# A narrower second top-16 search, ranks turned into key numbers by one operation per rank, and ScalarE's gelu moved one tile later

## The reference

```python
s1 = q[:, :, 0] @ sub_keys1.T        # 256 tokens, 8 heads, 128 keys
s2 = q[:, :, 1] @ sub_keys2.T
v1, i1 = lax.top_k(s1, 16)
v2, i2 = lax.top_k(s2, 16)
cand = v1[..., :, None] + v2[..., None, :]            # 16 x 16 sums per head
top, ci = lax.top_k(cand.reshape(..., 256), 16)
idx = i1[ci // 16] * 128 + i2[ci % 16]                # one of 16384 experts
gate = softmax(top)
act = gelu(x . expert_u[idx])
out = sum(gate * act * expert_v[idx])
```

## Time and profile before

| | us |
|---|---|
| median of 3 runs | 2029.18 |
| the profiled execution | 2028.88 |
| its span, first to last instruction | 2027.0 |
| TensorE (PE) busy | 2004.3 |
| VectorE (DVE) busy | 1488.2 |
| ScalarE (ACT) busy | 1061.8 |
| GpSimd (POOL) busy | 1029.8 |

### The profile page before, as it was taken

How to read it: one execution, slowest core, us unless ns; L and a number is a source line. 1 busy time by engine, 2 the same in 40 slices (tenths; PEclk the granted TensorE clock), 3 DMA queues, 4 the chain that set the end, 5 groups by cost and what they waited for, 6 DMA issues and landing times.

```text
span 2027.0 us, 39960 instructions
## 1 busy us (share of the span) xinstructions
PE 2004.3 (99%) x12788; PEld 1819.2 (90%) x12788; DVE 1488.2 (73%) x3096; ACT 1061.8 (52%) x1746; POOL 1029.8 (51%) x425
## 2 busy tenths in 40 slices
PE   9999999999999999999999999999999999999998
PEld 7999998899999888888889999888999998888887
DVE  2855169988887888888639450799888878888886
ACT  5644555567776333333466444555677753333333
POOL 6898779787775000000278988798777740000001
PEclk8999999999999999999999999999999999999999
DMA  8355557675666787878774556676666567787775
GB/s 256 129 194 188 183 186 235 212 226 198 197 195 195 244 239 242 242 240 242 240 208 143 192 174 199 194 235 215 213 197 199 197 203 243 240 241 241 241 242 175
DMA packets 172128, 429.62 MB, mean 212 GB/s; under 512 B 19156, under 2 KB 83957, under 8 KB 171510
## 3 DMA queue, kind: packets, MB, share of 16 engines
q1 hardware_dynamic: 171588, 425.56, 66.5%
q10 hardware_dynamic: 434, 2.63, 0.3%
HBM read 392.79 MB, written 35.32 MB: 211 GB/s over the span
## 4 chain that ended last, share of the span: by engine, by line
PE 93%; DVE 3%; issue 1%; POOL 1%; ACT 1%; DMA 1%; DVEq 0%; POOLq 0%; ACTq 0%; SPq 0%
PE bank L1300 40%; PE bank L1563 33%; PE bank L1549 9%; PE bank L1551 5%; PE bank L1614 3%; POOL halves L545 1%; PE bank L1529 1%; DVE area L1155 0%; DVE area L1159 0%; DVE area L1162 0%; PE bank L1439 0%; DMA ring<-in_stream 0%; PE bank L1395 0%; DVE act L1235 0%; DMA x<-in_x 0%
## 5 line engine op out<-in xcount | busy, mean ns | idle before, releaser
L545 POOL TENSOR_TENSOR halves<-ring,halves 128x1024 fp32r<-128x1024 f32 x412 | 1024.2, 2498 | 975.7 <-DVE coef L1243 683.0
L626 ACT ACTIVATE halves<-ring 128x1024 fp32r<-128x1024 f32 x668 | 705.2, 1057 | 684.7 <-PE bank L1563 414.1
L1300 PE MATMUL bank<-hT,halves 128*128 128x256 f32 x6048 | 751.8, 283 | 1.9 <-DVE hT L921 1.7
L1300 PEld LDWEIGHTS bank<-hT,halves 128*128 128x128 f32 x6048 | 737.2, 192 | 4.4 <-DVE hT L921 2.1
L1563 PE MATMUL bank<-halves,coef 128*128 128x512 f32 x3000 | 681.5, 389 | 0.0
L1563 PEld LDWEIGHTS bank<-halves,coef 128*128 128x128 f32 x3000 | 562.7, 188 | 117.4 <-issue 0.5
L1223 DVE TENSOR_TENSOR halves<-ring,halves 128x1024 fp32r<-128x1024 f32 x256 | 315.5, 1233 | 12.7 <-ACT halves L626 10.2
L1549 PE MATMUL bank<-hT,halves 128*128 128x512 f32 x896 | 312.2, 395 | 3.0 <-POOL halves L545 3.0
L1551 PE MATMUL bank<-hT,halves 128*128 128x256 f32 x896 | 248.6, 277 | 0.0
L1549 PEld LDWEIGHTS bank<-hT,halves 128*128 128x128 f32 x896 | 168.1, 188 | 42.7 <-issue 3.6
L1551 PEld LDWEIGHTS bank<-hT,halves 128*128 128x128 f32 x896 | 168.3, 188 | 0.0
(11 more groups left out here) (168 smaller groups left out, 1375.0 us busy)
## 6 DMA issues: line engine op xcount, KB each, us to landing
ring<-in_stream SPq DMA_DIRECT2D x668, 512.0 KB, 4.0
held_blocks<-act SPq DMA_DIRECT2D x244, 128.0 KB, 1.8
act<-held_blocks SPq DMA_DIRECT2D x244, 128.0 KB, 3.0
area<-rel_scratch SPq DMA_DIRECT2D x16, 128.0 KB, 5.4
area<-in_gains SPq DMA_DIRECT2D x4, 512.0 KB, 4.1
x_home<-x ACTq DMA_DIRECT2D x2, 1024.0 KB, 4.2
x<-x_home SPq DMA_DIRECT2D x2, 1024.0 KB, 8.0
area<-in_params SPq DMA_DIRECT2D x2, 640.0 KB, 7.6
```

Source lines behind the costliest of these rows:

```text
L545: pool.tensor_tensor(halves[:, s, 1, :], ring[:, s, :], halves[:, s, 0, :].bitcast(F32), ALU.subtract)\
L626: a.activation(halves[:, s, 0, :], ring[:, s, :], ACT.Copy).then_inc(hi_done, 1)
L1300: i = pe.matmul(o, stationary[a], moving[b], start=begin and n == 0, stop=end and n == len(TERMS) - 1)
```

## The change

The first of the two layers and the second are changed alike.

- **Sums.** Of the 16 x 16 sums of a head, 112 are formed: the first 4 ranks of the first list with all 16 of the second, and the other 12 with the first 4 (a sum at ranks a and b, counted from 1, has at least a x b - 1 sums not below it). Four additions take the place of two. The second search runs over 112 columns in place of 256.
- **Ranks.** With two kinds of rows the split of the index takes two shifts, three copies to float (in SBUF; the two of before went to PSUM) and four fused operations. A rank then becomes a number by 16 fused operations per list, each `(rank == r) * number r` on 256 elements for both token tiles, and two sums of 16 terms per list. 7 folds stand in this part where 12 stood.
- **ScalarE.** For tile n it makes the high side of tile n + 4 and then takes the gelu of tile n - 1. The exponential moves from ahead of the high side of tile 48 to behind that of tile 44 and the gelu of tile 39. The rounds behind it are written out where a loop was.

SP, GpSimd and TensorE have the code of before.

```diff
--- before.py
+++ after.py
@@ -78,7 +78,11 @@
 assert T_PU % RING == 0 and PARKED % RING == 0 and HELD % RING == 0 and NK % RING == 0 and TAIL == RING == 4
 MAIN = NK - EARLY
 GAIN_AT = 12
-EXP_AT = 11
+EXP_AT = 10
+WIDE = 4
+NARROW = 4
+CAND = WIDE * TOPK + (TOPK - WIDE) * NARROW
+assert (WIDE + 1) * (NARROW + 1) > TOPK and WIDE * TOPK == 64
 SEL_AT = 2
 assert SETS == HELD
 HIS = NT - 2
@@ -122,7 +126,7 @@
 NBANK = 8
 NGV = sum(who == "V" for _, who in PLAN)
 NGA = NG - NGV
-NCHAIN = 59
+NCHAIN = 54
 NROOT = 5
 
 
@@ -270,12 +274,13 @@
         row = part(TT, PH, 2, NK)
         val = part(TT, PH, 2, TOPK)
         idx = part(TT, PH, 2, TOPK, dt=U32)
-        cand = part(TT, PH, TOPK, TOPK)
+        cand = part(TT, PH, CAND)
         top = part(TT, PH, TOPK)
         ci = part(TT, PH, TOPK, dt=U32)
         ca = part(TT, PH, TOPK, dt=U32)
         cb = part(TT, PH, TOPK, dt=U32)
-        eq = part(PH, TOPK, TOPK)
+        eq = part(TOPK, S)
+        caf, cbf = part(S), part(S)
         sel = part(3, TT, P)
         summed = part(2, S)
         used[0] = max(used[0], used_mix)
@@ -294,7 +299,7 @@
         key1T, key2T = (bank[0][:, c * S:(c + 1) * S] for c in range(2))
         weightT, weight_low = (bank[1][:, c * S:(c + 1) * S] for c in range(2))
         idf = bank[6][:, :].rearrange("p (t h c r) -> p t h c r", t=TT, h=PH, c=2)
-        caf, cbf = (bank[7][:, c * S:(c + 1) * S].rearrange("p (t h r) -> p t h r", t=TT, h=PH) for c in range(2))
+        c0, c4, c2 = (eq[:, n, :] for n in range(3))
 
         act_row = act[:, :, :].rearrange("p s t -> p (s t)")
         relv = act_row[0:HEADS, 0:NDIST]
@@ -777,19 +782,39 @@
                 high_up_to(T_PU + RING - 1)
 
                 a.activation(stat[:, 13:14], one, ACT.Gelu_apprx_tanh)
-                def turn(r, s):
+                def next_high(r, s):
 
                     a.wait_ge(tiles_used, l * NT + r * RING + (T_PU + s + 1))
                     high(r * RING + (T_PU + RING + s), s)
-                    park(r, s)
-
-                with a.Fori(0, EXP_AT) as r:
+
+                def turn(r, s):
+
+                    next_high(r, s)
+                    if s > 0:
+                        park(r, s - 1)
+                    else:
+                        park_last(r)
+
+                def park_last(r):
+
+                    a.wait_ge(sides_added, l * PARKED + r * RING)
+                    a.wait_ge(held_stored[1], l * (8 * (EARLY - 2)) + r * (8 * RING))
+                    a.activation(act[:, 1, :], summed[:, 1, :], ACT.Gelu_apprx_tanh).then_inc(act_done, 1)
+
+                next_high(0, 0)
+                for s in range(1, RING):
+                    turn(0, s)
+                with a.Fori(1, EXP_AT) as r:
                     for s in range(RING):
                         turn(r, s)
+                next_high(EXP_AT, 0)
+                park_last(EXP_AT)
                 a.wait_ge(shifted_ready, l + 1)
                 a.activation(sel[:, 2], sel[:, 2], ACT.Exp).then_inc(gexp_ready, 1)
                 a.activation(stat[:, 13:14], one, ACT.Gelu_apprx_tanh)
-                with a.Fori(EXP_AT, PARKED // RING - 1) as r:
+                for s in range(1, RING):
+                    turn(EXP_AT, s)
+                for r in range(EXP_AT + 1, PARKED // RING - 1):
                     for s in range(RING):
                         turn(r, s)
                 for s in range(RING):
@@ -801,6 +826,7 @@
                         a.activation(weight[:, :, :], weight_hi.bitcast(F32).rearrange("p (n u) -> p n u", u=FOUR)[:, :, 2:],
                                      ACT.Copy).then_inc(weights_hi, 1)
                     turn(PARKED // RING - 1, s)
+                park_last(PARKED // RING)
 
                 def hold(i):
 
@@ -1112,14 +1138,16 @@
 
                 for t in range(TT):
                     fold()
-                    i = v.tensor_tensor(cand[:, t], val[:, t, :, 0, :].unsqueeze(3).to_broadcast([P, PH, TOPK, TOPK]),
-                                        val[:, t, :, 1, :].unsqueeze(2).to_broadcast([P, PH, TOPK, TOPK]), ALU.add)
+                    for a0, many, width, at in ((0, WIDE, TOPK, 0), (WIDE, TOPK - WIDE, NARROW, WIDE * TOPK)):
+                        sums = cand[:, t, :, at:at + many * width].rearrange("p h (a b) -> p h a b", a=many)
+                        i = v.tensor_tensor(sums, val[:, t, :, 0, a0:a0 + many].unsqueeze(3).to_broadcast([P, PH, many, width]),
+                                            val[:, t, :, 1, 0:width].unsqueeze(2).to_broadcast([P, PH, many, width]), ALU.add)
                 then_search(i)
                 fold()
                 pairs = [(t, h) for t in range(TT) for h in range(PH)]
                 for k in range(2):
                     ks = slice(8 * k, 8 * k + 8)
-                    flat = [cand[:, t, h].rearrange("p a b -> p (a b)") for t, h in pairs]
+                    flat = [cand[:, t, h, :] for t, h in pairs]
                     for n, ((t, h), f) in enumerate(zip(pairs, flat)):
                         i = v.max(top[:, t, h, ks], f)
                         if n < len(pairs) - 1:
@@ -1144,23 +1172,31 @@
                     i = v.tensor_tensor(gate[:, t], top[:, t], top[:, t, :, 0:1].to_broadcast([P, PH, TOPK]), ALU.subtract)
                 i.then_inc(shifted_ready, 1)
 
-                v.tensor_scalar(ca.rearrange("p t h j -> p (t h j)"), ci.rearrange("p t h j -> p (t h j)"), 4, None,
-                                ALU.logical_shift_right)
-                link(v.tensor_scalar(cb.rearrange("p t h j -> p (t h j)"), ci.rearrange("p t h j -> p (t h j)"), 15, None,
-                                     ALU.bitwise_and))
-                v.tensor_copy(caf.rearrange("p t h r -> p (t h r)"), ca.rearrange("p t h r -> p (t h r)"))
-                link(v.tensor_copy(cbf.rearrange("p t h r -> p (t h r)"), cb.rearrange("p t h r -> p (t h r)")))
+                flat = [z.rearrange("p t h j -> p (t h j)") for z in (ci, ca, cb)]
+                v.tensor_scalar(flat[1], flat[0], 4, None, ALU.logical_shift_right)
+                link(v.tensor_scalar(flat[2], flat[0], 2, None, ALU.logical_shift_right))
+                for o, z in zip((c0, c4, c2), flat):
+                    i = v.tensor_copy(o, z)
+                link(i)
+                fold()
+                link(v.scalar_tensor_tensor(caf, c2, float(WIDE - WIDE * TOPK // NARROW), c4, ALU.add, ALU.max))
+                v.scalar_tensor_tensor(c4, caf, -float(TOPK), c0, ALU.mult, ALU.add)
+                link(v.scalar_tensor_tensor(c2, caf, -float(NARROW), c0, ALU.mult, ALU.add))
+                link(v.scalar_tensor_tensor(cbf, c2, float(WIDE * NARROW - WIDE * TOPK), c4, ALU.add, ALU.max))
                 for c, rank in ((0, caf), (1, cbf)):
+                    for r in range(TOPK):
+                        numbers = idf[:, :, :, c, r].rearrange("p t h -> p (t h)").unsqueeze(2).to_broadcast([P, TT * PH, TOPK])
+                        i = v.scalar_tensor_tensor(eq[:, r, :].rearrange("p (h j) -> p h j", j=TOPK), rank.rearrange("p (h j) -> p h j", j=TOPK),
+                                                   float(r), numbers, ALU.is_equal, ALU.mult)
+                        if r % 6 == 5:
+                            fold()
+                    link(i)
                     for t in range(TT):
-                        link(v.tensor_tensor(eq, rank[:, t].unsqueeze(3).to_broadcast([P, PH, TOPK, TOPK]),
-                                             iota[:, 0:TOPK].unsqueeze(1).unsqueeze(1).to_broadcast([P, PH, TOPK, TOPK]),
-                                             ALU.is_equal))
-                        fold()
-                        link(v.tensor_tensor(eq, eq, idf[:, t, :, c, :].unsqueeze(2).to_broadcast([P, PH, TOPK, TOPK]),
-                                             ALU.mult))
-                        fold()
-                        link(v.tensor_reduce(sel[:, c, t].rearrange("p (h j) -> p h j", h=PH), eq, AX.X, ALU.add))
-                        fold()
+                        i = v.tensor_reduce(sel[:, c, t], eq[:, :, t * P:(t + 1) * P].rearrange("p r j -> p j r"), AX.X, ALU.add)
+                        if t == 0:
+                            fold()
+                    link(i)
+                assert EXP_AT * RING <= folds[0] <= PARKED - 2, folds[0]
                 v.wait_ge(gexp_ready, l + 1)
                 gs = small[:, 0:16].rearrange("p (t h) -> p t h", t=TT)
                 link(v.tensor_reduce(gs, gate, AX.X, ALU.add))
```

## The result

The kernel after takes a median of **2057.79 us** (2056.1 to 2059.16, 4 runs) beside 2029.64 us (2028.71 to 2030.52, 4 runs) for the kernel before: a ratio of 1.0138, 95% interval 1.0121 to 1.0156. That is 28 us slower, where the forecast said 12; the time lies 0.8 us above the end of the range. The profiled execution took 2059.16 us, its span is 2057.3, 30.3 above the span of before.

The account below looks back on a forecast made before the run. TensorE, busy 99% of the span, was taken as the bound. Loop, exponential, one-hots and part 2 gave 9.5 us a layer against 2.7, +6.8, taken as 5.9: +11.8 in two layers, 2041.0 us, range 2026 to 2057.

Parts of the forecast that it names:

- The bound: TensorE's gaps in the parked tiles, 2.7 us a layer and 5.4 in all, are the most the change can gain.
- Part 1: Search over 112 sums on VectorE: saves 16 us of VectorE a layer, worth nothing on TensorE.
- rival D: Search of 112 columns costs as one of 256: 12 us of VectorE stay, time as forecast; no chance of its own.
- Part 2: Ranks to numbers on VectorE: 7 folds for 12 and operations behind GpSimd make TensorE wait 1.5 us a layer.
- Part 3: Gelu one tile later on ScalarE delays SP's stores and the loads behind them; expected to decide the time.
- the loop: High side, gelu, store, load, high side two tiles on: 5.83 us against TensorE's 5.56, losing 0.27 per pair.
- The steps from tile 35: Sign in the parked tiles: TensorE waits for GpSimd's low sides in steps from about tile 35, above all behind the exponential.
- The exponential: Moved to tile 44 on ScalarE: finds its input ready, costs 3.4 us less 1.5 of slack, so 2.0 a layer.
- C: Rival, much slower: VectorE's operations behind GpSimd lose 8 us more, or layer 1 keeps 4.2 us landings; 2053 us, chance 0.21.
- B: Rival, no change: loads land about 3.4 us after issue, lateness stays inside the lead; 2029 to 2030 us, chance 0.17.
- A: Rival, faster: loads land within 3.3 us, late starts never add up; 2024.8 us, chance 0.12.

Follow-up runs that it names:

- the best version: Kernel before with 112 sums, 15 folds for 19 ahead of the shifted gates, 15 for 12 behind, exponential ahead of tile 40's high side: 2024.81 us, ratio 0.9977.

## Why the prediction was right or wrong

**The bound: nearly right.** The gaps were 2.7 us a layer, and the best version took 2.5 to 2.6 out of each parked stretch. But that is 1.84 of gaps and 0.7 of busy time behind them, which the bound left out; the 0.9 at the one-hots stayed.

**Part 1: right in its worth, wrong in its size.** Index, maximum and replacement fell from 419 to 269, 413 to 259 and about 410 to 258 ns: 12 us, as worked out, and rival D is refuted. But the four sums took 7.5 us (estimated 2.0), three of the four behind low sides of GpSimd. It did not matter: the folds are pinned in the program, and VectorE's spare time became waiting. Ahead of its folds it stood idle for 30.7 us, where the earlier trace rows have 11.8:

```profile
L1101 DVE TENSOR_REDUCE area<-bank 128x256 f32<-128x512 f32 x56 | 38.4, 688 | 30.7 <-ACT act L780 17.5 <-PE bank L1587 6.8 <-ACT act L802 5.6
```

**Part 2: the step that failed.** The sum's term for part 2 was 1.5 us a layer; VectorE's part alone cost 9 (18.4 in all). The forecast had the right wait, 7 folds in a section too long for four banks, but made the section 32.5 us from the shift on, where 38.1 were measured, and charged too little for its length. Three errors lie on top of each other, beside the count of folds itself (below).

- The four sums over ranks were taken at the 2.28 us of another layout of the terms. They measured 3.8: 6.1 us a layer that no row of before could show, but for which a bound ("another distance between terms") should have stood.
- The 3 us for operations behind GpSimd measured 3.3 (copies 1.8 over their estimate, first fused 1.5), and the subtraction ahead of them another 1.3. Their size was nearly right, but they were priced at 0.5 us. The banks' cover was already used up, so by the forecast's own rule 3 us of VectorE cost 3 us of TensorE. That was an error of arithmetic.
- The sum had each gap at its length, while behind some of them the clock fell to half for a few us. For VectorE's part alone that is 2.8 us of the 9 in each parked stretch.

The rule of part 2 ranks the kernels with 7 folds against the rest, and no more. Written for a section that is measured from the subtraction on, TensorE waits for its length + 1.5 - 0.9 - 2.78 for each fold and one more - 7.3 of cover. The gaps measured stand in two columns, since a second wait shows beside the one for folds:

| kernel | section, us | folds | by the rule | gaps ahead of the transposes | at the transposes |
|---|---|---|---|---|---|
| before | 40.6 | 12 | below 0 | 1.5 (exponential) | 0.3 |
| after | 39.9 | 7 | 11.0 | 9.7 / 7.8 | 0 |
| after, later store | 41.3 | 7 | 12.4 | 8.1 / 7.9 | 0 |
| VectorE's part alone | 39.4 | 7 | 10.5 | 8.2 / 7.9 | 0 |
| before with 7 folds | 37.3 | 7 | 8.4 | 6.6 / 6.5 | 0 |
| VectorE's part, 11 folds | 41.7 | 11 | 1.7 | 0.4 / 0.5 | 2.5 / 2.4 |
| 112 sums, new split | 44.9 | 13 | below 0 | 3.0 | 1.7 |
| the same, exponential earlier | 44.2 | 13 | below 0 | 0 | 5.9 |
| before, exponential earlier | 40.5 | 12 | below 0 | 0 | 2.4 |
| shift behind fold 36 | 47.4 | 15 | below 0 | 0 | 0 |

For the kernels with 7 folds the rule is 1 to 4.5 us too high. With the forecast's own 29.5 + 3 us, and 0.6 for the subtraction, it gives 4.2, not 1.5.

Where the folds are close enough, the section's end decides: the transposes ahead of tile 54 need it. The shift starts 111.8 us behind the first parked matmul, and 54 tiles at 2.775 us end at 149.9. So a section behind fold 40 may last about 38 us. The two kernels that have an earlier exponential and no other gap fit that: 44.2 and 40.5 us would make 6.2 and 2.5 of waiting, and 5.9 and 2.4 were measured. With the shift behind fold 36, 100.7 us in, a section of 47.4 is over in time.

**The missing folds, not the slow sums, are the root.** The kernel before, with none of the new operations, lost 15 us by 7 folds for 12; the change's own operations lost 5.7 with 11. Five folds are 13.9 us of TensorE's pace. Most of what is left there are the 2.5 / 2.4 us at the transposes, the section's length.

**Part 3: mechanism right, place wrong, the size in part luck.** Two of the signs named came: waits for `ring<-in_stream` in dozens of places (46 in a layer) and 4.2 / 2.7 us at the one-hots for the 3.9 foretold. One sign was badly put: the load comes 2.1 us, not 6, behind the high side that sets it off; it is the whole loop that takes 5.8.

What the forecast gave the loop, the exponential and the one-hots together was 8.0 against 2.7, +5.3 a layer; on top of VectorE's part the late gelu cost 9.9 us in both layers, 5.0 each. That the two agree is luck: 2.1 of the 8.0 were to be gaps in the loop and 2.0 the exponential, and the trace has no such gap but one of 0.2 in layer 1, while the lower clock behind the one-hots was not in the sum. By itself the late gelu showed 2.7 a layer in its own stretches.

The steps from tile 35 did not come in the kernel after: loads landed a median of 3.4 us after issue, not 3.6, in both layers, so the loop takes 5.63 us where 5.56 are to be had. TensorE met VectorE's folds at tile 47 first; only ScalarE's part alone showed such a wait earlier, 1.2 and 0.5 us at tile 26. Layer 1's 4.2 us did shrink, as forecast, but the reason given, a slower pace, is not shown: other kernels had shorter landings at the old pace (last section). By the Trainium skill (DMA: Bandwidth & Descriptors, section "Anatomy of one DMA — SWDGE (gpsimd) path") the estimate was 3.2 us and no waiting at all; the 3.4 us measured are still on the other side. That section's fit is for transfers that GpSimd issues. These are issued by SP, so it need not hold for them.

**The exponential: right in its input, wrong in its price.** It ran at 387.48, behind the gelu of tile 39 and its table load, and waited for nothing. Of the 2.0 us that it was to cost nothing shows in layer 0, where TensorE has no gap before tile 47, and 0.2 in layer 1. The experiments add what was overlooked: with the exponential out of the way the transposes are next.

**The rivals.** C came nearest in size (2053, 4.8 us short) and had the right engine: VectorE late beyond the banks' cover. Its cause was only partly the right one: of what the section took beyond the forecast, the operations behind GpSimd are 4.6 us and the distance of the terms is 6.1.

Twelve folds in place of 7 would have made the section 43.0 us long; that was not run, and by the 38 us above about 5 us of waiting would have come at the transposes, an estimate.

B's condition, a landing of about 3.4 us, is what came, and so did its loop: lateness that TensorE does not see. B failed by what it gave to VectorE's folds and to the last wait. A is refuted: the loads did not land in time. One part of its result, TensorE without the exponential's gap, was reached by the kernels with the exponential earlier, but without a new gap only by moving the shift to fold 36.

## What to carry to other kernels

Where one engine's long work is interleaved by hand with short work that another engine waits for, count the short pieces per us of the section against the consumer's pace, first of all, and then the section's end against the point where its result is needed. Work saved between them was worth nothing here until they were spaced anew, and once the cover is spent nearly every further us is paid: of two kernels with the early exponential, the one with a section longer by 3.7 us waited 3.5 more. When an operation is moved later, read what stands behind it on every queue that it releases: here a store ahead of a load.

## What the runs showed of the hardware

- A sum over 16 terms of 4 bytes, 2048 in all, takes 2.28 us with the terms side by side and 3.8 us with them 1 KB apart. A fused operation of 256 elements takes 411 ns when it writes them side by side and 614 ns when 64 bytes apart.
- In the kernel after, TensorE's clock fell to half for a few us behind gaps of 1.8 to 4.2 us, but not behind each: not behind those of 2.50 and 2.67 us in layer 0, where the granted clock stayed at 1.00. Nor did it fall behind those of 1.0 and 1.2 us.
- VectorE's short operations behind the shift took 0.28 to 0.43 us, and up to 2.6 us when they began during a low side of GpSimd. In five kernels (before, after, VectorE's part alone, and the two with the shift at fold 36), 34 of the 35 that read all of their input from SBUF, and read two inputs or wrote SBUF too, ended 0.15 to 0.30 us behind the low side. Six others that began during one had PSUM as an input or took a single input into PSUM; none of them waited.
- The loads of layer 1 landed a median of 4.2 us after issue in the kernel before and 3.4 in the kernel after. The spacing does not explain it: they also landed in 3.5 in the kernel before with 7 folds, at the old pace of a load every 2.75 us. The kernel after with the later store had 4.3 again. The cause is open.
- Open: in some profiled executions the untouched token mixers took 3 us more in a layer (225.8 for 222.8), with one wait for VectorE longer by 1.3 us and a lower clock behind it. First the row of the kernel before with the exponential one round earlier (196 to 222), then that of the kernel before:

```profile
196.00:222.00 26.00, 23.02 (x116) 19.20 (x115) 14.27 (x16) 14.03 (x25) 15.17 (x7) 0.93 0.45 159
```

```profile
196.00:222.00 26.00, 24.33 (x140) 20.71 (x139) 12.31 (x16) 15.27 (x27) 16.82 (x8) 1.00 0.51 174
```

It came with 3.0 us in both layers of ScalarE's part alone, about 6 of that kernel's 12 us. The version with terms side by side and the one with 112 sums and the earlier exponential had 3.0 and 1.5 us; in one layer alone came 3.0 us with 11 folds and with the earlier exponential on the kernel before, and 1.5 or 1.6 with 112 sums, with the later store, and with ScalarE's part and the later store. The kernel after, VectorE's part alone, the kernel before with 7 folds and both kernels with the shift at fold 36 had none. So a difference of 3 us between two kernels need not come from the stretch that was changed. What sets it off wasn't found.
